# Modulation vectors accumulated as four column quarters on four partition quarters, in a two-block transformer kernel

## The reference

```python
c_act = jax.nn.silu(c)
for i in range(DEPTH):                      # first stack, N_MOD = 9
    mod = c_act @ ada_w[i] + ada_b[i]
    sh1, sc1, g1, sh2, sc2, g2, sh3, sc3, g3 = jnp.split(mod, N_MOD, axis=-1)
    h = modulate(rms_norm(x, ln_ffn1[i]), sh1, sc1)
    x = x + 0.5 * g1[:, None, :] * swiglu(h, ffn1_wg[i], ffn1_wu[i], ffn1_wd[i])
...
c_act = jax.nn.silu(c)
for layer in range(DEPTH):                  # second stack
    mod = c_act @ ada_w[layer] + ada_b[layer]
    sh1, sc1, g1, sh2, sc2, g2 = [m[:, None, :] for m in jnp.split(mod, 6, axis=-1)]
...
```

## Time and profile before

| | before |
|---|---|
| median of 3 runs | 1808.8 us (1805.85 to 1808.93) |
| span of the profiled execution | 1806.0 us |
| TensorE busy | 1747.5 us, 97% |
| VectorE busy | 1382.4 us, 77% |
| ScalarE busy | 912.2 us, 51% |
| GpSimd busy | 261.5 us, 14% |
| moved by DMA | 411.42 MB, 228 GB/s over the span |

### The profile page before, as it was taken

One profiled execution on the slowest core, in us unless ns is written; L12 is line 12 of the kernel. 1 busy time (PEld: TensorE's weight loads), 2 busy tenths in 40 slices (PEclk: granted clock), 3 DMA queues, 4 the chain that ended last, 5 costly groups with the idle time before them and its releaser, 6 DMA issues. The chain is left out here.

```text
span 1806.0 us, 35803 instructions
## 1 busy us (share of the span) xinstructions
PE 1747.5 (97%) x14215; PEld 1709.8 (95%) x14215; DVE 1382.4 (77%) x1621; ACT 912.2 (51%) x1267; POOL 261.5 (14%) x423
## 2 busy tenths in 40 slices
PE   6999999999999999999999999899999998899999
PEld 5999999999999999989999998899999997699999
DVE  6767798687668877767967789769888898778555
ACT  3433377763335433456533366566444556655443
POOL 1411110011002011010110134411110121200000
PEclk9999999999999999999999999999999998999999
DMA  9988857459876888746697847335889492137450
GB/s 347 372 305 277 298 171 256 152 176 327 298 270 233 281 286 289 261 176 221 239 320 258 298 160 252 106 121 198 298 301 286 136 242 98 48 129 256 166 184 24
DMA packets 256071, 411.42 MB, mean 228 GB/s; under 512 B 17975, under 2 KB 200801, under 8 KB 255841
## 3 DMA queue, kind: packets, MB, share of 16 engines
q1 hardware_dynamic: 223032, 290.79, 49.2%
q0 software_dynamic: 32432, 119.04, 17.7%
q10 hardware_dynamic: 504, 0.18, 0.0%
HBM read 408.90 MB, written 2.63 MB: 228 GB/s over the span
## 5 line engine op out<-in xcount | busy, mean ns | idle before, releaser
L2678 DVE TENSOR_TENSOR lo<-raw,hi 128x2048 fp32r<-128x2048 f32 (+1 forms) x257 | 582.0, 2267 | 234.5 <-ACT hi L2512 234.0
L2512 ACT CAST hi<-raw 128x2048 fp32r<-128x2048 f32 (+1 forms) x266 | 498.4, 1876 | 387.2 <-PE dacc L2244 186.1
L2242 PE MATMUL up<-operand_hi,hi 128*128 128x256 f32 x1952 | 554.4, 284 | 3.6 <-DVE lo L2678 3.6
L2243 PE MATMUL up<-operand_lo,hi 128*128 128x256 f32 x1952 | 553.8, 284 | 0.0
L2244 PE MATMUL up<-operand_hi,lo 128*128 128x256 f32 x1952 | 553.6, 284 | 0.0
L2242 PEld LDWEIGHTS up<-operand_hi,hi 128*128 128x128 f32 x1952 | 375.9, 193 | 4.5 <-DVE lo L2678 4.4
L2243 PEld LDWEIGHTS up<-operand_lo,hi 128*128 128x128 f32 x1952 | 376.0, 193 | 0.0
L2244 PEld LDWEIGHTS up<-operand_hi,lo 128*128 128x128 f32 x1952 | 375.9, 193 | 0.0
L2242 PE MATMUL dacc<-act_hi,hi 128*128 128x256 f32 x1056 | 300.6, 285 | 3.4 <-DVE act_lo L2891 3.4
L2244 PE MATMUL dacc<-act_hi,lo 128*128 128x256 f32 x1056 | 299.8, 284 | 0.0
L2243 PE MATMUL dacc<-act_lo,hi 128*128 128x256 f32 x1056 | 299.2, 283 | 0.0
(11 more groups left out here) (432 smaller groups left out, 2784.4 us busy)
## 6 DMA issues: line engine op xcount, KB each, us to landing
ada<-in_ada_w_dram POOLq DMA_DIRECT2D x224, 512.0 KB, 6.0
raw<-in_ffn_wg_dram SPq DMA_DIRECT2D x88, 512.0 KB, 4.9
raw<-in_ffn_wu_dram SPq DMA_DIRECT2D x88, 512.0 KB, 5.3
raw<-in_ffn_wd_dram SPq DMA_DIRECT2D x88, 512.0 KB, 5.1
raw<-in_ffn_w_up_dram SPq DMA_DIRECT2D x88, 512.0 KB, 4.5
raw<-in_ffn_w_down_dram SPq DMA_DIRECT2D x46, 512.0 KB, 4.4
raw<-in_hg_w_in_dram SPq DMA_DIRECT2D x32, 512.0 KB, 6.0
raw<-in_attn_w_qkv_dram SPq DMA_DIRECT2D x24, 512.0 KB, 7.0
```

The source lines that it names most:

```text
L2242: pe.matmul(o, stat[0], mov[0], start=start, stop=False, skip_group_check=True)
L2243: pe.matmul(o, stat[0], mov[1], start=False, stop=False, skip_group_check=True)
L2512: last = act.copy(put(slab(hi, s, SPL)), take(slab(raw, s, RAW)))
L2678: last = dve.tensor_tensor(put(slab(lo, s, SPL)), take(slab(raw, s, RAW)), put(slab(hi, s, SPL)).bitcast(F32), ALU.subtract)
```

## The change

Partitions and columns are regrouped. A tile still has 128 rows of the matrix by 1024 columns, but partition quarter g (32 partitions) now holds column quarter g (256 columns) of all 128 rows, in four pieces side by side: partition 32g + q, piece j has row 32j + q. So a tile is loaded by four DMAs, one for each partition quarter, and accumulated by four passes of 256 columns, one for each piece j, into an accumulator of 128x256. Each partition quarter then has its own 256 outputs, and the sum over partitions takes two matmuls with a moving operand of four columns, `group_ones`, which has ones in quarter g of column g. `c` is laid out to match: 32 columns for each stack instead of 8, the same 32 numbers in each partition quarter.

```diff
+AG = 4
+AW = D // AG
+AQ = P // AG
+ASTEPS = KB * AG
...
-            return view(8192, 9216) if v == 1 else ada_acc
+            return view(8192, 8192 + AW) if v == 1 else ada_acc[:, 0:AW]
...
+            source = ada_source(v, k) if source is None else source
+            for g in range(AG):
+                eng.dma_start(ada_place(m)[g * AQ:(g + 1) * AQ, :].rearrange("q (j n) -> q j n", j=AG),
+                              source[:, g * AW:(g + 1) * AW].rearrange("(j q) n -> q j n", q=AQ)).then_inc(full, 16)
...
+            link(pool.memset(group_ones[:, :], 0.0))
+            for g in range(AG):
+                link(pool.memset(group_ones[g * AQ:(g + 1) * AQ, g:g + 1], 1.0))
...
-                for k in range(KB):
-                    last = pe.matmul(o[:, k:k + 1], acc_of(v)[:, k * P:(k + 1) * P], ones[:, 0:1],
+                by_group = o[:, 0:KB].rearrange("p (g h) -> p g h", g=AG)
+                for h in range(KB // AG):
+                    last = pe.matmul(by_group[:, :, h], acc_of(v)[:, h * P:(h + 1) * P], group_ones[:, :],
                                      start=True, stop=True, skip_group_check=True)
...
+                for j in range(AG):
+                    t = ada_place(m)[:, j * AW:(j + 1) * AW]
+                    i = (ASTEPS if v >= V2 else 0) + k * AG + j
+                    c = c_col[:, i:i + 1]
+                    if k == 0 and j == 0:
+                        dve.tensor_scalar(acc, t, c, None, ALU.mult).then_inc(S["ada_step"], 1)
+                    else:
+                        dve.wait_ge(S["ada_step"], AG * m + j + ASTEPS * it)
+                        dve.scalar_tensor_tensor(acc, t, c, acc, ALU.mult, ALU.add).then_inc(S["ada_step"], 1)
```

## The result

| | before | after |
|---|---|---|
| median | 1808.9 us (4 runs, 1805.85 to 1810.88) | 1930.5 us (4 runs, 1920.04 to 1935.33) |
| span of the profiled execution | 1806.0 us | 1918.1 us |
| TensorE busy | 1747.5 us | 1740.2 us |
| VectorE busy | 1382.4 us | 1550.0 us |
| GpSimd busy | 261.5 us | 629.7 us |

The ratio is 1.0664, 95% interval 1.0630 to 1.0698: 122 us slower, far above the range of 1796 to 1860. The sign and the duration of the narrow passes were forecast; the size was not.

The account below looks back on a forecast made before the run. TensorE was taken to bound the rounds, with VectorE 7 to 10 us to spare. Added costs of 39.8 less 35.3 from the shorter sum gave +4.5 on 1806.0, so 1810.5, as median 1813 us; range 1796 to 1860.

Parts of the forecast that it names:

- The sign: Whole kernel: slower than before, given a chance of 0.53, against 0.28 for faster and 0.19 for no change.
- waits for tiles: Loop rounds: some wait for tiles that land late in their four places, 0.4 x 16 = 6.4 us.
- the walk: C0 round stepped through by engine: tile 7 issued at 15.1, needed at 23.4; landing takes 9.2 us against 8.3.
- a lag of 12 to 17 us: Loops: slabs, loaded six ahead, can lag two or three; 6 us a phase fit in, made good at its end.
- Rival 3: Tiles come too late, GpSimd's ring shared with SP's; F-loop rounds of 37.5 us, total 1853 us; chance 0.17.
- Rival 1: Tile and slab loads overlap on both rings and cost little; total 1798 us; chance 0.22.
- Rival 2: A register ahead of each wait makes loop passes cost 0.63 us each; total 1859 us; chance 0.08.
- The start: Program start, two vectors accumulated in a row: 11 us more, the vector F0 waits for at 49 instead of 38.1.
- The sum: TensorE's sum over partitions falls from 1.68 to 0.42 us; 28 vectors save 35.3 us, the start's sum 2.6.
- The passes: VectorE's four quarter passes a tile, 0.515 us apart, add 6.4 us a vector in a loop.
- Outside the loops: Iterations 1 and 2, with eight tiles in less time, and A, H: C0 4.2, C1 3.0, F1 to F3 0.8 each.
- the likeliest case: Whole kernel: all terms as summed, 1813 us; chance 0.45 of landing within 8 us.

Follow-up runs that it names:

- e4: Changed kernel with each of a tile's four DMAs writing one column quarter into all 128 partitions, instead of 32 neighbouring ones: 1840.7 us.
- e1: Kernel before with only the four narrow tile loads of the change, old passes and sum kept: 1882.5 us.
- e6: Changed kernel with a tile's four DMAs issued in the order of quarters 0, 2, 1, 3: 1889.7 us.
- e9: Changed kernel with only the start's 16 tiles loaded by one full-width DMA each: 1909.3 us.
- e2: Changed kernel with each tile loaded by one full-width DMA as before, four passes and short sum kept: 1827.1 us.
- e3: Kernel before with only the sum shortened to two matmuls of four columns, passes and loads as before: 1778.2 us.
- e8: Against the changed kernel: two column halves on even and odd partitions, two passes of 512, four matmuls, two full-width DMAs a tile: 1803.1 us.

## Why the prediction was wrong

**The step that failed is the price of late tiles.** The prediction put "waits for tiles" at 0.4 x 16 = 6.4 us and all that the narrow loads cost at 11.4; they cost 90. The 0.4 has no working: in the walk tile 7 came 0.9 us late against a reserve of 1.2. The rates behind it were near: 218 GB/s for narrow loads, where 236 were measured in the start, and 36.6 us of DMA in a round, where 10.48 MB at 263 to 282 GB/s take 37 to 40. The walk for a tile was near too: 9.2 us from its first issue to its landing, where the median from the first of four issues to the last landing is 9.7 (6.1 in e4). But the spread was left out, which reaches 12.3 us in F1, and so was the number: not tile 7 alone is late but some three tiles a round (11 waits in the loop of F0, 12 in that of F1; 0.85, 0.53 and 1.71 us in the round shown). VectorE waits for tiles 17.0 us in the loop of F0, 13.7, 10.8 and 10.1 in F1 to F3 and 4.3 in C0. What TensorE waits for `lo` after that is 42 us, where e4 has 4.3, all in C0.

The slabs, for which the prediction allowed a lag of 12 to 17 us to be made good at a phase's end, landed in over 9 us and not 5, but within the loops nothing waited for one. Six places covered them there, as it said; the tiles have four. Between the profiled executions of the changed kernel and of e4 lie 73 us: 59 in the five loops, 11 ahead of F0's first round, 4 in G. The 263 to 282 GB/s are no fixed rate of the mixture either: e1's rounds of F0 moved the same bytes at 275 and 299 GB/s in 36.3 to 36.4 us, with TensorE full. In that loop VectorE, with its old passes, waited for tiles 22.9 us and TensorE for VectorE only 0.5. Later in e1 slabs were late too: ScalarE waited for them 12.8 us in the loop of F1 and 10.4 in that of F3.

**Rival 3 named the right mechanism**: rounds of 37.5 were forecast, and F1's second and third are 37.4 and 37.6. It was given 0.17 and 40 us. It fell short by the long first rounds (40 to 42), by phase G, which took 5.5 us more, and by the start. Rival 1 (the rings overlap, 1798) had more weight and is refuted: the changed kernel's rounds moved 263 to 282 GB/s, no more than the 286 that the prediction's 36.6 us without any overlap make. Within one ring there seems to be some, since e6 gives back 41 of 90 us by the order of issue. Rival 2 (0.63 a pass in loops) is refuted by 0.517; its sum also took 2.0 us a round where its own terms, 3.6 less 1.2, make 2.4.

**The start** was put at +11 with 49 us for the vector. It came at 54.7. Two things were missed: SP's 48 further issues stand ahead of F0's up slab, and ScalarE waits for that slab before it scales. With e9 the start's loads are 21 us. The sum's part there came true: 3.41 us became 0.85 for the second vector. The prediction's "half clock" is not in the view of before, which gives 1.00 for that stretch; what it shows is 0.21 us a row, twice the 0.105 of the loops. In the changed kernel the view gives 0.50 there, with the same 0.21.

**The passes** were right where they were walked: step 0.515 (0.517), F's rounds 35.07 (35.0 in e2), C0's rounds 36.2 (36.7). Not walked was the end of each loop. "Outside the loops" counted iterations 1 and 2 only. Behind the last round the sum and the last down slab are due 23.5 us after the sum before, and VectorE, which had 2.7 us of idle time there, has 6.4 more: 5.0 us in the F1 shown, and 6 to 7 in a phase together with iterations 1 and 2 (e2 against e3: F1 6.9, F2 6.5, F3 6.3). Some 5 for each of five loops is 25, against the 19 by which the passes were sized too low.

**The sum** gave 1.3 us a vector in every loop, against 1.26 forecast (rounds 36.3 to 35.0; F1 6.3 for five vectors in e3), and 30.2 in all. F0 was 7.8 shorter, as counted; F2, F3 and C0 5.3 to 5.7 each, and A, H, C1 nothing that can be told from the spread of a phase, where a us of TensorE is not a us of the phase.

**The direction** held: slower had 0.53. With a likeliest time only 4 us above the kernel before, and terms of +11.4 and +29.7 that measured +90 and +49, this is luck more than foresight. The range ended at 1860 because the likeliest case and rival 2 set its top. Rival 3 itself had no dear end, though a share near 1 means that every later stretch inherits the shortage.

## What to carry to other kernels

When an edit brings the DMA engines from a share of 0.84 to 1, ask first which stream has the fewest places: here the tiles, with four, were late in every loop, while nothing in the loops of the changed kernel waited for a slab, with six. Take the spread of their landings and not the median, and follow each late tile to the work that stands behind it. Before a tile is split over partition groups, look at which partitions one DMA writes: interleaved groups cost here 77 us less than blocks of neighbours, with the same arithmetic. And walk the last round of a loop apart from the others, since what follows it wants its results sooner than a next round would.

## What the chip showed that was not expected

- Loads into 32 neighbouring partitions run at 236 GB/s and into alternating blocks of 64 at 260, both with a share of 1.07 to 1.08; full-width ones at 397 with one issue a tile, and at 271 with four, but then with a share of 0.90. What was not expected is that they hold the engines for the others too: full-width slabs beside them landed in 9.9 us and not 4.9.
- The order in which four narrow DMAs stand in a queue is worth 41 us (0, 2, 1, 3 against 0, 1, 2, 3).
- scalar_tensor_tensor on 128 partitions in SBUF lasts 285, 485, 759 and 1285 ns for 64, 256, 512 and 1024 columns: some 0.22 us and 1.04 ns a column. The Trainium skill, page "VectorE: DVE Perf Modes", section "The TRN2 errata", advises 512 elements or more; here two passes of 512 were worth their price (e8) and four of 256 were not (e2).
